# A two-layer hybrid encoder on one core: other norms, router products and token list

## The reference, cut to what matters

```
for l in 0, 1:
    h = rmsnorm(x) * (1 + sc1) + sh1
    z = h @ w_in                    # mLSTM | indexer and attention | pooling
    x = x + g1 * (concat(mlstm, attention, pool) @ w_out)
    h = rmsnorm(x) * (1 + sc2) + sh2
    layer 0: f = (silu(h @ w1) * (h @ w3)) @ w2
    layer 1: logits = h @ w_router + b_router; top 2 of 8 experts, softmax gates
             f = sum over the two chosen experts of gate * swiglu_expert(h)
    x = x + g2 * f
y = rmsnorm(x)
```

## Time and profile before

| what | value |
|---|---|
| median of 3 runs | 2808.49 us (2805.67 to 2822.73) |
| profiled execution, its own time | 2808.37 us |
| its span, first to last instruction | 2806.8 us |
| PE, DVE, ACT, POOL busy | 84%, 55%, 41%, 6% of the span |
| granted clock, mean | 0.859 |
| DMA | 485.02 MB, mean 173 GB/s |

### The profile page before, as it was taken

One profiled execution on the slowest core, in us unless ns is written; L12 is line 12 of the kernel. 1 busy time (PEld: TensorE's weight loads), 2 busy tenths in 40 slices (PEclk: granted clock), 3 DMA queues, 4 the chain that ended last, 5 costly groups with the idle time before them and its releaser, 6 DMA issues. The chain is left out here.

```text
span 2806.8 us, 37886 instructions
## 1 busy us (share of the span) xinstructions
PE 2358.6 (84%) x14277; PEld 2016.5 (72%) x14277; DVE 1536.5 (55%) x2169; ACT 1163.2 (41%) x1554; POOL 180.9 (6%) x265
## 2 busy tenths in 40 slices
PE   6799985769799999969998677863999999999973
PEld 3799753548699999969985444752878787787852
DVE  0456637232444344543664542323888888888863
ACT  3332114231433342333211332222777777777753
POOL 2000001110000000000000201102000000000011
PEclk7799767659899999988995775875999999999986
DMA  8222523232545354511231504006999999999962
GB/s 261 78 73 64 173 79 112 81 116 70 144 140 147 119 170 122 163 45 61 63 96 61 190 28 146 24 25 154 325 371 359 357 380 344 373 358 347 377 238 78
DMA packets 286363, 485.02 MB, mean 173 GB/s; under 512 B 22430, under 2 KB 217512, under 8 KB 286240
## 3 DMA queue, kind: packets, MB, share of 16 engines
q1 hardware_dynamic: 264816, 416.42, 43.5%
q0 software_dynamic: 21424, 66.86, 7.1%
HBM read 455.73 MB, written 26.98 MB: 172 GB/s over the span
## 5 line engine op out<-in xcount | busy, mean ns | idle before, releaser
L840 PE MATMUL banks<-upper_parts,region_split 128*128 128x320 f32 x1664 | 397.0, 314 | 34.7 <-DVE weights_lower L2032 34.7
L2032 DVE TENSOR_TENSOR expert_lower<-expert_ring,region_split 128x1408 fp32r<-128x1408 f32 (+1 forms) x270 | 388.1, 1468 | 64.6 <-ACT region_split L1544 57.5
L840 PE MATMUL banks<-region_split 128*128 128x320 f32 (+1 forms) x1376 | 378.0, 338 | 27.8 <-DVE region L2032 14.8
L840 PE MATMUL banks<-upper_parts,weights_lower 128*128 128x320 f32 x1248 | 391.9, 314 | 0.0
L1544 ACT ACTIVATE region_split<-expert_ring 128x1408 fp32r<-128x1408 f32 (+1 forms) x270 | 331.2, 1256 | 100.7 <-DMA expert_ring<-in_we 100.5
L840 PEld LDWEIGHTS banks<-upper_parts,region_split 128*128 128x128 f32 x1664 | 289.6, 192 | 36.6 <-DVE weights_lower L2032 36.6
L840 PE MATMUL banks<-region_split,upper_parts 128*128 128x512 f32 (+1 forms) x996 | 300.7, 378 | 1.4 <-DVE upper_parts L2032 1.4
L840 PEld LDWEIGHTS banks<-region_split 128*128 128x128 f32 x1376 | 245.3, 189 | 48.1 <-issue 32.8
L840 PE MATMUL banks<-z_weights_upper,upper_parts 128*128 128x256 f32 (+3 forms) x844 | 261.2, 341 | 14.5 <-DVE region_split L2032 14.5
L840 PE MATMUL banks<-expert_lower,upper_parts 128*128 128x512 f32 x720 | 269.4, 374 | 0.0
L1544 ACT ACTIVATE region_split<-weight_ring 128x2048 fp32r<-128x2048 f32 (+2 forms) x72 | 141.0, 1960 | 252.4 <-PE banks L840 225.1
(11 more groups left out here) (287 smaller groups left out, 3685.3 us busy)
## 6 DMA issues: line engine op xcount, KB each, us to landing
expert_ring<-in_we SPq DMA_DIRECT2D x240, 704.0 KB, 8.2
expert_ring<-in_we SPq DMA_DIRECT2D x165, 512.0 KB, 4.5
weight_ring<-in_w_ada SPq DMA_DIRECT2D x48, 1024.0 KB, 7.1
weight_ring<-in_w SPq DMA_DIRECT2D x88, 512.0 KB, 4.9
weight_ring<-in_w_in SPq DMA_DIRECT2D x24, 1024.0 KB, 5.2
weight_ring<-in_w SPq DMA_DIRECT2D x16, 1408.0 KB, 6.3
weight_ring<-in_w_out SPq DMA_DIRECT2D x8, 1024.0 KB, 9.5
y_rows<-hidden_t POOLq DMA_DIRECT2D x15, 512.0 KB, 7.6
```

What stands on the lines that cost most here:

```text
L840: return nc.tensor.matmul(out, lhsT, rhs, start=first, stop=last)
L2032: return v.tensor_tensor(out, x, y, op)
```

## The change

- **Norms.** DVE sums four squared tiles at a time; PE makes the sum over partitions with the sums stationary and one column of ones moving, so tokens lie on partitions: 5 columns instead of 640. Root and reciprocal are of 128 x 5. DVE spreads the result on a diagonal (`DIAG`), and PE multiplies ones by it, which puts the factor for each token into every partition of PSUM. Sample tokens of all k are done at once (`sample_norm`). Before z there is no barrier between norm and split: each tile is split once it is modulated.
- **Modulation chunks.** None stand beside the norms. Layer 0: mlstm 5, index 5, sample attention 8, pool 6. Layer 1: 5, 3, 8, 0. In the sample attention both steps use bank 7.
- **Router.** Its constants load after the out stage. The weights, padded to 32 columns, are stationary and the tokens moving, four tiles k in four column groups; ACT copies the result, and five products by `SUM4` turn it.
- **Masks and ranks.** The masks no longer wait for the exponential; DVE makes running sums of them (`MSUM`), and the ranks take 3 products.
- **Token list.** DVE makes one-hot rows of each copy's pass and of its place in the pass; PE multiplies them (10 products), which gives a table of tokens by slot in SBUF. POOL copies a column for each pass; the scatter and the 16 loads are gone.

```diff
-ADA_LATER = [{"norm1": 4, "mlstm": 5, "index": 4, "pool": 6, "norm2": 5},
-             {"norm1": 0, "mlstm": 5, "index": 5, "pool": 6, "norm2": 0}]
-ADA_MIX = [x["mlstm"] + x["index"] + x["pool"] for x in ADA_LATER]
-assert ADA_FIRST + sum(sum(x.values()) for x in ADA_LATER) == 24 * DEPTH
+ADA_LATER = [{"mlstm": 5, "index": 5, "sample_att": 8, "pool": 6}, {"mlstm": 5, "index": 3, "sample_att": 8, "pool": 0}]
+ADA_MIX = [sum(x.values()) for x in ADA_LATER]
...
+                    pool.wait_ge(table_ready, 1)
...
-                    def gather(at, landed):
-                        pool.dma_start(IDX[:, :], by_slot[at, :, :].rearrange("i p o -> p (i o)")).then_inc(pass_tokens_in, 16)
-                        pool.wait_ge(pass_tokens_in, landed)
+                    def gather(at, known):
+                        nc.gpsimd.tensor_copy(IDX[:, :], TABLE[:, at]).then_inc(tokens_copied, 1)
+                        pool.wait_ge(tokens_copied, known)
...
-            def norm(name, chunks=0):
-                claim(0, 1)
-                for k in range(KD):
-                    take(squares_ready)
-                    mm(PS[:, 0, :], ones[:, :], HT[:, k, 0:TP], k == 0, k == KD - 1)
-                    ins = mm(PS[:, 1, 0:P], ones[:, :], HT[:, k, SAMPLE], k == 0, k == KD - 1)
-                hand(ins, "act", 0, 1)
-                ada(NORM_ROWS, chunks)
-                stage(name)
+            def norm():
+                claim(5)
+                for k in (0, 4):
+                    take(squares_summed)
+                    for t in range(NT):
+                        ins = mm(PS[:, 5, t:t + 1], HT[:, k, tiles(t)], ones[:, 0:1], k == t == 0, k == 4 and t == NT - 1)
+                hand(ins, "act", 5)
+                claim(6, 7)
+                take(diag_ready)
+                mm(PS[:, 6, :], ones[:, :], DIAG[:, 0:NTP, :].rearrange("p t j -> p (t j)"), True, True)
+                hand(mm(PS[:, 7, 0:P], ones[:, :], DIAG[:, NTP, :], True, True), "dve", 6, 7)
...
+                        if 1 <= u <= ADA_LATER[l]["sample_att"]:
+                            ada_turn(SAMPLE_ROWS, 7)
...
+                    if u < ADA_LATER[l]["sample_att"]:
+                        ada_products(7)
...
...
+                    take(router_in, 112)
+                    claim(0, 1)
+                    for k in range(KD):
+                        at = slice(32 * (k % 4), 32 * (k % 4 + 1))
+                        mm(PS[at, 0, :], WRT[:, k, :], HT[:, k, 0:TP], k < 4, k >= 4)
+                    for k in range(KD):
+                        at = slice(32 * (k % 4), 32 * (k % 4 + 1))
+                        ins = mm(PS[at, 1, 0:P], WRT[:, k, :], HT[:, k, SAMPLE], k < 4, k >= 4)
+                    hand(ins, "act", 0, 1)
...
-                        if t == 0:
-                            take(router_in, 80)
-                            claim(0)
-                            for u in range(NT):
-                                for k in range(KD):
-                                    ins = mm(PS[:, 0, u * NE:(u + 1) * NE], HT[:, k, tiles(u)], WRT[:, k, :],
-                                             k == 0, k == KD - 1)
-                            hand(ins, "dve", 0)
+                    turn_hidden(0)
+                    take(logits_out)
+                    claim(2)
+                    for t in range(NT):
+                        ins = mm(PS[:, 2, t * NE:(t + 1) * NE], LOGT[:, tiles(t)], SUM4[:, 0:NE], True, True)
+                    hand(ins, "dve", 2)
+                    turn_hidden(1)
+                    turn_hidden(2)
                     take(masks_ready)
-                    claim(1)
-                    for t in range(NT):
-                        out = PS[:, 1, t * NE:(t + 1) * NE]
-                        for u in range(t):
-                            mm(out, ones[:, :], MS[:, u, :], u == 0, False)
-                        mm(out, BEFORE[:, :], MS[:, t, :], t == 0, True)
-                    for u in range(NT):
-                        ins = mm(PS[:, 1, 64:64 + NE], ones[:, :], MS[:, u, :], u == 0, u == NT - 1)
-                    hand(ins, "dve", 1)
+                    claim(3)
+                    mm(PS[:, 3, 0:NT * NE], BEFORE[:, :], MS[:, :, :].rearrange("p t e -> p (t e)"), True, False)
+                    mm(PS[:, 3, 0:NT * NE], ones[:, :], MSUM[:, 0:NT, :].rearrange("p t e -> p (t e)"), False, True)
+                    hand(mm(PS[:, 3, 64:64 + NE], ones[:, :], MSUM[:, NT, :], True, True), "dve", 3)
+                    turn_hidden(3)
+                    turn_hidden(4)
+                    take(one_hots_ready)
+                    claim(0)
+                    for i in range(2):
+                        for t in range(NT):
+                            ins = mm(PS[:, 0, 0:MAX_PASSES], OF_REST[:, i, t, :], OF_PASS[:, i, t, :], i == t == 0, i == 1 and t == NT - 1)
+                    hand(ins, "dve", 0)
...
+            def root():
                 for k in range(KD):
                     func(HT[:, k, :], XT[:, k, :], ACT.Square).then_inc(squares_ready, 1)
                 take(for_act)
-                func(RS[:, 0:TP], PS[:, 0, :], ACT.Sqrt, scale=1.0 / D, bias=eps[:, 0:1])
-                drained(func(RS[:, SAMPLE], PS[:, 1, 0:P], ACT.Sqrt, scale=1.0 / D, bias=eps[:, 0:1]))
+                drained(func(ROOT, PS[:, 5, 0:NT], ACT.Sqrt, scale=1.0 / D, bias=eps[:, 0:1]))
                 also(root_ready)
...
+                root()
                 upper(0)
                 for k in range(KD):
-                    copy(ZH[:, k, :], HT[:, k, :]).then_inc(z_hidden_rounded, 1)
+                    modulate(k, mod(l, 1, k)[:, 0:1], mod(l, 0, k)[:, 0:1])
+                    if k == 1:
+                        act.wait_ge(sample_modulated, 2 * l + 1)
+                    if k:
+                        upper_hidden(k - 1)
+                upper_hidden(KD - 1)
...
+                    if 1 <= u < NB and u <= ADA_LATER[l]["sample_att"]:
+                        ada_vectors(ada_done, 7)
+                        ada_done += 1
...
+            def diagonal(gains):
+                for k in (0, 4):
+                    take(squares_ready, 2)
+                    link(tt(HT[:, k, :], HT[:, k, :], HT[:, k + 1, :], ALU.add))
+                    take(squares_ready, 2)
+                    link(tt(HT[:, k + 2, :], HT[:, k + 2, :], HT[:, k + 3, :], ALU.add))
+                    tt(HT[:, k, :], HT[:, k, :], HT[:, k + 2, :], ALU.add).then_inc(squares_summed, 1)
+                link(tt(XGS.rearrange("p k (b t) -> p k b t", t=TS), XT[:, :, SAMPLE].rearrange("p k (b t) -> p k b t", t=TS),
+                        gains, ALU.mult))
                 take(root_ready)
-                link(v.reciprocal(RS[:, :], RS[:, :]))
+                link(v.reciprocal(ROOT, ROOT))
+                tt(DIAG[:, :, :], along(ident[:, :], 1, NT), along(ROOT, 2, P), ALU.mult).then_inc(diag_ready, 1)
+            def scale(k):
+                if k >= 2:
+                    take(modulated)
+                tt(NT2[:, k % 2, :], XT[:, k, 0:TP], PS[:, 6, :], ALU.mult).then_inc(scaled_ready, 1)
+            def sample_norm(shifts):
+                row = along(PS[:, 7, 0:P], 1, KD)
+                if shifts is None:
+                    tt(HT[:, :, SAMPLE], XGS, row, ALU.mult).then_inc(sample_modulated, 1)
+                else:
+                    link(tt(XGS, XGS, row, ALU.mult))
+                    tt(HT[:, :, SAMPLE].rearrange("p k (b t) -> p k b t", t=TS), XGS.rearrange("p k (b t) -> p k b t", t=TS),
+                       shifts, ALU.add).then_inc(sample_modulated, 1)
+            def scaled():
+                also(dve_drained)
+                n.add("dve_drained")
+                n.add("modulated", 2)
+            def norm(gains, shifts):
+                diagonal(gains)
+                take(for_dve)
                 for k in range(KD):
-                    if k >= 2:
-                        dve.wait_ge(modulated, n.value("modulated") + k - 1)
...
+                diagonal(sample_vectors(l, 1))
+                lower(0)
+                take(for_dve)
+                for k in range(KD):
+                    scale(k)
+                    if k == 1:
+                        sample_norm(sample_vectors(l, 0))
+                    if k >= 2:
+                        lower_hidden(k - 2)
+                scaled()
+                lower_hidden(KD - 2)
+                lower_hidden(KD - 1)
...
-                    take(pair_exp_ready)
+                    copy(MS[:, :, :], RMK[:, :, :])
+                    v.memset(MSUM[:, 0, :], 0.0)
                     link(tt(RMK[:, :, :], RMK[:, :, :], RM2[:, :, NE:], ALU.subtract))
-                    tt(MS[:, :, :], RMK[:, :, :], RM2[:, :, NE:], ALU.add).then_inc(masks_ready, 1)
-                    link(v.tensor_scalar(GA[:, :], E2[:, :], 1.0, None, ALU.add))
-                    link(v.reciprocal(GA[:, :], GA[:, :]))
-                    link(tt(GB[:, :], GA[:, :], E2[:, :], ALU.mult))
```

(67 more changed lines are left out.)

149 lines of the change are left out of this document (78 added, 71 removed).

## The result

The changed kernel takes 2702.88 us, the median of four runs (2696.46 to 2707.33); the kernel before, run beside it, 2807.08 (2803.74 to 2822.73). The ratio of all their executions is 0.9616, 95% interval 0.9575 to 0.9658 (the two medians alone give 0.963): 104 us faster. 68 were forecast, and the range (2715 to 2762) doesn't hold the time. The profiled execution has a span of 2694.8 us where the one of before had 2806.8, so the two traces have 112.0 us to tell apart.

A forecast was written before the change was run, and what follows sets the result against it. No single engine was taken to bound the whole; chains of engines taking turns counted. -37.8 - 22.2 - 19.4 - 1 - 12.0 + 24 = -68.4 us, from 2808.4 to 2740; forecast 2728 to 2752, range 2715 to 2762.

The forecast's parts named there:

- The modulation chunks: Chunks moved between stages: layer 1's pool loses six, -12.0 us; eight per layer in sample attention cost +24 us.
- with gaps filled the sample attention would run at the high clock: Rival on sample attention: chunks cost nearly nothing, +9.6 instead of +24 us, gather perhaps uncontended; 2721 us, chance 0.17.
- a clock that falls for longer stretches: Sign of being wrong, for the chains: every term is priced at one of two clock levels; no size given.
- The norms: Five norm chains, from first square to first consumer: shortened to 24 us or less, 30 before z; -37.8 us together.
- Router and slots: From the router's logits through masks and ranks to the slots: earlier logits, fewer waits, -22.2 us together.
- Column groups: Router logits on TensorE: eight 640-column products in four column groups take 4.9 us.
- The one-hot products: After the slots are known: ten TensorE products for the token table, 0.51 us each at the low clock, 5.1 us.
- the gather: Before the first expert product: with weight rows in flight, the gather lands 9.3 us after issue.
- the list: From slots to first expert product: token table made in SBUF, 23.9 us where it was 43.3, -19.4 us.
- the expert stage does not follow: Rival on the expert stage: the weight stream sets its end, so -19.4 shrinks to some 5 us; 2754 us, chance 0.05.
- The chunks of the pool stage: Layer 1's pool stage loses six modulation chunks, so its transposes start sooner: -12.0 us.
- Slower than before: Rival on sample attention: chunk loads land behind keys and values and all stop; 2850 us at 7 us a chunk, chance 0.02.

## Why the prediction was wrong

The difference between -112.0 and -68.4 is 43.6 us. The table splits it: sample attention 35.1 (-11.1 for +24), norms 8.5 (-46.3 for -37.8), router and slots 5.0, experts 2.2, pool 0.4, and against them 7.6 in stretches for which nothing was forecast. Against the median of the measured times (-104) it is 36 us, since the profiled execution was a quick one.

**The step that failed** is the price of the sample attention under *The modulation chunks*, "with clock 0.61 nearer to the upper end: +24"; the runs showed -11.1 in its place. I took the clock of the window before as given and priced only what was added. The clock depends on the work: with the products added, every other product of the stage runs at or near 1.0 too (0.93 on average in layer 1), and TensorE's own 111 us in the two stages are most of what can shrink. Put -11 in the place of +24 and the same sum gives 2705, where 2703 was measured. That they lie so close is partly luck: -11 is read from the quickest execution, the norms gave 8.5 us more than forecast, and the index stage is at the low clock in some executions. The edit with the keys ahead, at -14 each, shows what the step was worth without the wait for loads.

**The rival that came nearest** had 0.17: "with gaps filled the sample attention would run at the high clock". Its mechanism is the right one and its price was wrong by the same mistake. It priced the added products at the high clock (+9.6), and not the stage. I weighed it down with the pool stage, where the same products ran at 0.50 with TensorE busy throughout. That row is true and is seen again (0.50 in the pool stage of 57.1 us above), but it says nothing about these products in another surrounding. The Trainium skill (TensorE: Matmul & The Clock Gate, "What's actually happening") holds that activity releases the throttle. By that rule the chunks give the stage the high clock, and the sample attention agrees: 0.57 to 0.93. The indexer, busy 24.40 of 24.40 us at 0.50, does not show it, nor does the second part of layer 0's sample attention, busy 29.29 of 29.90 us at 0.53.

The prediction's own sign of being wrong was "a clock that falls for longer stretches". The clock that decided rose.

**The norms** were right in their mechanism and a little large in three terms: from first square to first consumer 22.6 and 22.5 us where I had 24.0, 20.8 for 22.3 in the last one, 29.4 for 29.8 before z (1205.67 to 1235.03). The first norm of layer 0 with its z gave 1.3 us more than forecast, and the store behind the last norm 2.1 that I hadn't looked at.

**Router and slots.** Column groups as priced (4.50 for 4.9, at the low clock). VectorE had the logits 2.7 us sooner than forecast, because the clock rose behind them: the first eight transposes took 1.16 us and not 1.97, the five turns 1.28 and not 2.6. The one-hot products took 4.46 for 5.1, the gather 8.4 for 9.3. Undoing the list costs 19.8 us where I had 19.4 for it, and the rival that the expert stage does not follow is out.

**The chunks of the pool stage** gave 12.4 for 12.0.

**Slower than before** could come from a chunk's load that lands late. No wait for `w_ada` stands in either sample attention; the harm came another way: keys and values landed late, and the 2.8 us of waiting in layer 0 cost 15.3 us in all, 12.5 of them through the clock. The window has 196 GB/s and not 85, but the loads need not be the whole cause. With eight products and no chunk loaded, the quicker stage also waits for such a load, once, for 0.9 us, and layer 1 at 241 GB/s waits twice for only 0.4. I had looked for late chunks and not for late keys.

## What to carry to other kernels

Before pricing what is added to a stage that runs at the low clock, ask what its own products would take at the high one: real work put into TensorE's gaps can shorten the stage by more than it costs, and useless work shows in one cheap run whether it would. Then look for the waits for loads in that stretch, for one of 1.6 us cost 12.9 here. A term priced by the clock of the window before needs two values, one for each clock, for all the work in the window.

## What was not expected of the hardware

- Eight products of no use in each step made the sample attentions 16.6 and 19.2 us shorter (67.3 and 68.4 to 50.7 and 49.2), sixteen 12.4 and 13.8.
- TensorE was busy 24.40 of 24.40 us with products of 64 rows at a granted clock of 0.50, and in other executions did them at 1.00 in 12.40. With useless products ahead of them the clock fell from 1.00 within them in both layers, behind the same 0.94 us of idle time as where it held. What decides is not settled; single times of one kernel lie up to 33 us apart (2698.93 to 2731.69).
- The four units of the indexer take 12.51 us one behind the other and 3.93 each, 15.7 together, with other products between them, at the same clock of 1.00. In layer 1 of the profile with chunks between them the last two units stand side by side and take 6.79, so a unit behind another adds 2.86. That neighbouring units run partly beside one another, since they use different halves of the rows, would explain it; it was not tried by itself.
